# Three gate/up pages, not two, issued ahead of the next expert's upper down half

## The reference

```python
gu = xblk @ w_gate_up[e] + b_gate_up[e]              # (tokens, 1024) @ (1024, 2048)
x_glu = jnp.minimum(gu[:, :D_EXPERT], SWIGLU_LIMIT)
x_lin = jnp.clip(gu[:, D_EXPERT:], -SWIGLU_LIMIT, SWIGLU_LIMIT)
act = x_glu * jax.nn.sigmoid(SWIGLU_ALPHA * x_glu) * (x_lin + 1)
return act @ w_down[e] + b_down[e]                   # (tokens, 1024) @ (1024, 1024)
```

## Time and profile before

| | |
|---|---|
| median of 3 runs | 1222.7 us (1222.44 to 1223.84) |
| the profiled execution: its own time, its span | 1223.64 us, 1221.8 us |
| PE busy, DVE, ACT, POOL | 1032.7 us (85%), 289.0, 188.9, 31.6 |
| moved | 465.42 MB, 381 GB/s over the span |
| mean granted clock of TensorE | 0.943 |
| chain that ended last | PE 50%, DMA 39%, of which the down weights 35% |

### The profile page before, as it was taken

How to read it: one execution, slowest core, us unless ns; L and a number is a source line. 1 busy time by engine, 2 the same in 40 slices (tenths; PEclk the granted TensorE clock), 3 DMA queues, 4 the chain that set the end, 5 groups by cost and what they waited for, 6 DMA issues and landing times.

```text
span 1221.8 us, 21400 instructions
## 1 busy us (share of the span) xinstructions
PE 1032.7 (85%) x8279; PEld 504.9 (41%) x8280; DVE 289.0 (24%) x786; ACT 188.9 (15%) x459; POOL 31.6 (3%) x55
## 2 busy tenths in 40 slices
PE   2799999987785999979898899889888979696966
PEld 1565888743342334324443444334334333233333
DVE  6646522142121111202121212111211121111112
ACT  0311345041110101101110111111111111010102
POOL 1000200230000000000000000000000000000000
PEclk9799999997798999989998999999999999898989
DMA  9979730988999979999999999999999999999996
GB/s 352 385 272 402 292 135 6 407 316 351 426 425 426 426 288 380 425 426 418 411 423 425 403 427 425 425 401 426 425 427 396 427 426 427 423 426 425 425 426 259
DMA packets 60000, 465.42 MB, mean 381 GB/s; under 512 B 5342, under 2 KB 7430, under 8 KB 27084
## 3 DMA queue, kind: packets, MB, share of 16 engines
q1 hardware_dynamic: 59212, 462.50, 91.8%
q0 software_dynamic: 480, 1.59, 0.4%
q10 hardware_dynamic: 288, 1.05, 0.2%
HBM read 463.01 MB, written 2.11 MB: 381 GB/s over the span
## 4 chain that ended last, share of the span: by engine, by line
PE 50%; DMA 39%; DVE 5%; issue 3%; ACT 2%; POOL 1%; DVEq 0%; SPq 0%; ACTq 0%; POOLq 0%
DMA arena<-in_w_down_dram 35%; PE pp L1398 14%; PE pp L1427 14%; PE pp L1195 4%; DMA arena<-in_w_ada_dram 4%; PE pp L1117 2%; PE pp L1362 2%; PE pp L1208 2%; PE po L1260 2%; PE po L1343 2%; DVE arena L757 2%; PE pp L1371 1%; PE pp L1377 1%; ACT work L674 1%; PE po L1075 1%
## 5 line engine op out<-in xcount | busy, mean ns | idle before, releaser
L1398 PE MATMUL pp<-arena,work 128*32 128x256 f32 (+1 forms) x3840 | 376.5, 448 | 20.3 <-ACT work L674 20.3
L1427 PE MATMUL pp<-arena,work 128*32 128x256 f32 (+1 forms) x1920 | 205.8, 477 | 78.6 <-DMA arena<-in_w_down_dram 78.6
L1398 PEld LDWEIGHTS pp<-arena,work 128*32 128x32 f32 (+1 forms) x3840 | 165.9, 118 | 214.8 <-issue 129.8
L1427 PEld LDWEIGHTS pp<-arena,work 128*32 128x32 f32 (+1 forms) x1920 | 80.4, 128 | 185.6 <-DMA arena<-in_w_down_dram 90.9
L979 DVE TENSOR_SCALAR work<-pp 128x128 f32<-128x128 f32 (+1 forms) x74 | 24.9, 337 | 405.3 <-PE pp L1398 405.3
L1362 PE MATMUL pp<-h_sb,work 128*32 128x256 f32 (+1 forms) x480 | 59.6, 461 | 36.0 <-issue 31.5
L677 ACT ACTIVATE work<-work 128x128 f32<-128x128 f32 (+1 forms) x74 | 25.9, 350 | 405.3 <-DVE work L979 405.3
L973 DVE COPY work<-pp 128x256 f32<-128x256 f32 (+1 forms) x37 | 19.4, 525 | 255.2 <-PE pp L1362 255.2
L1343 PE MATMUL po<-work 64*128 64x512 f32 x304 | 75.5, 615 | 1.2 <-ACT work L693 1.2
L1195 PE MATMUL pp<-arena 128*128 128x256 f32 x256 | 57.4, 382 | 0.0
L757 DVE SCALAR_TENSOR_TENSOR arena<-arena,small 128x1024 f32<-128x1024 f32 x42 | 54.0, 1285 | 8.5 <-DMA arena<-in_w_ada_dram 7.0
(11 more groups left out here) (208 smaller groups left out, 650.2 us busy)
## 6 DMA issues: line engine op xcount, KB each, us to landing
arena<-in_w_gate_up_dram SPq DMA_DIRECT2D x128, 2048.0 KB, 26.8
arena<-in_w_down_dram SPq DMA_DIRECT2D x64, 2048.0 KB, 24.5
arena<-in_w_ada_dram SPq DMA_DIRECT2D x12, 2048.0 KB, 12.5
arena<-in_w_in_dram SPq DMA_DIRECT2D x5, 2048.0 KB, 15.5
arena<-in_w_gate_dram SPq DMA_DIRECT2D x4, 2048.0 KB, 14.3
arena<-in_w_out_dram SPq DMA_DIRECT2D x2, 2048.0 KB, 10.0
arena<-in_w_branch_a_dram SPq DMA_DIRECT2D x1, 2048.0 KB, 18.6
arena<-in_w_branch_b_dram SPq DMA_DIRECT2D x1, 2048.0 KB, 17.4
```

Source lines behind the costliest of these rows:

```text
L1398: mm = t_.matmul(pp[j * m:(j + 1) * m, UP[hh], 0:w].rearrange("p (s f) -> p s f", s=2), hgT[:, at:at + m], gu_w[slot][:, k, :, r * PAIR:(r ...
L1427: mm = t_.matmul(pp[j * m:(j + 1) * m, UP[0], 0:w], actT[:, at:at + m], wd[:, j * w:(j + 1) * w], start=(n == 0), stop=(n == KD - 1))
```

## The change

In each pass of SP's loop the third gate/up page (number 2) of place n + 2 is issued before the wait for the end of place n, behind a wait of its own for that page to be free, and no longer after the upper down half of place n + 1. The number of transfers and their sizes are the same. Nothing else is changed; the issues ahead of the loop and after it are as they were.

```diff
@@ -428,12 +428,13 @@
                     load_gu(slot, e, 0)
                     sp.wait_ge(s_gfree, total * 3 + 1)
                     load_gu(slot, e, 1)
+                    sp.wait_ge(s_gfree, total * 3 + 2)
+                    load_gu(slot, e, 2)
                     sp.wait_ge(s_y, total)
                     load_dhi(last_e)
                     sp.reg_mov(dhi_expert, e)
                     load_bgu(slot, e)
-                    for q in range(2, 4):
-                        load_gu(slot, e, q)
+                    load_gu(slot, e, 3)
                     load_dlo(slot, e)
                     count_blocks(i * 2 + (1 + slot))
```

## The result

1239.41 us (median of 4, 1238.71 to 1239.69) against 1223.27 us for the kernel before (4 runs): ratio 1.0128, 95% interval 1.0115 to 1.0140. The change makes the kernel 16.1 us slower; 1240.7 was forecast. The profiled execution has a span of 1237.4 us, 15.6 more than before.

A forecast was written before the change was run, and what follows sets the result against it. The expert loop was taken to stream weight pages at 4.98 us each, PE waiting for hi; 4.3 + 14.0 + 0 − 0.3 = +18.0 us on 1222.7 gave 1240.7 us, range 1234 to 1246.

The forecast's parts named there:

- Term 1: From place 3 on, each hi (upper down half) lands one page later in the queue: +4.3 us.
- Term 2: Places 9, 13, 17, 21: a new 4.0 us dry stretch of the queue, +3.5 us each, +14.0 us in all.
- The cycle's bounds: Delay per dry stretch in places 9, 13, 17, 21: 2.8 us if cheap, 4.2 us if slow.
- term 4: At the end, the last hi comes early against PE, so the last block's remaining wait goes: −0.3 us.
- Term 3: Place 5: the first gap grows to 7 us, the second shrinks to about 5, hi(6) as today: 0.

## Why the prediction was right

*Term 1 (4.3).* hi(3) lands 4.2 us later than before; the last eight passes, undone, give 4.8 back. That 4.2 meets 4.3 to a tenth is partly luck. The two traces differ by 1.2 us before the change has done anything: hi(0), issued ahead of the loop, lands at 276.52 + 12.1 = 288.6, and at 275.60 + 11.8 = 287.4 before. How much of this is in the 4.2 isn't shown, so the term is known to about 1 us.

*Term 2 (14.0).* From hi(9) to hi(10) 33.6 us instead of 30.3. The landings of the other three pairs give 33.8, 33.75 and 33.7 where the kernel before has 30.4, 30.35 and 30.3; the four add 13.6. The sum's two numbers were 11.14 us from hi to the issue of g0 (now 11.15) and 7.7 us for a page from an empty queue (7.7 again). The estimate of 6.8 us, from the fit in the Trainium skill (DMA: Bandwidth & Descriptors, Anatomy of one DMA) for transfers issued by GpSimd, isn't what SP's queue shows. The cycle's bounds were 2.8 and 4.2; the prediction doesn't say how it gets 2.8, and its upper sum of 21.8 leaves out term 4.

*Term 3 (0).* hi(5) lands at 405.57 + 24.17 = 429.74; hi(6) is issued at 463.70 into an empty queue and lands 7.8 us later, 41.8 us after hi(5), as before. The gaps were to be 7 and 5, and are 6.2 and 4.3.

*Term 4 (−0.3).* There is no wait in the last down product any more, its 64 products run through:

```profile
1221.99 3.66 PE L1428 MATMUL pp<-arena,work 128*32 128x256 f32 x64
```

They end at 1225.65, where those of before ended at 1210.14, +15.5.

What the sum has too much is 1.9 us on the median. The terms measured, 4.2 + 13.6 − 0.3 = 17.5, come 2 us above the +15.5 at the end of the last product. The difference lies in the streaming stretches between: each of the five from one hi to a later one (3 to 5, 10 to 13, 14 to 17, 18 to 21, 22 to 30) took 0.3 to 0.6 us less than before, 1.8 together (6 to 9 took 0.1 more). A page time of 4.98 for both orders was assumed there; in this trace it is slightly less, and I have no cause for it.

Two forecasts of the profile were off. PE's wait for hi grew to 92.6 and not 97. The largest part of what is missing is at place 3, where it grew by 1.7 us and not by 4.3, since PE was itself 2.5 us later there: y(2), which releases hi(3), is at 352.32 instead of 349.86.

```profile
370.48 4.49 PE L1428 MATMUL pp<-arena,work 128*32 128x256 f32 x48 [3.12 <-DMA arena<-in_w_down_dram]
```

The waits at places 12, 16, 20 and 24 grew by 4.8, 4.7, 3.1 and 3.3 us, where 3.5 each was forecast. And y(3) came at 375.18 instead of 373.6, since 48 products after the longer wait in place 3 took 4.49 us and not 2.80; it cost nothing, for hi(4) is bound by the queue.

## What to carry to other kernels

In one ordered queue that is full, a transfer issued earlier is another one that lands later. Before moving one ahead, look at who waits for the transfer that it passes, and at what stands behind that one while the next page's buffer is still in use; the gain comes only where the queue is about to run dry and the passed transfer has slack. Here the page issued early cost 16 us in all passes and gained some 7 to 8 in five of them, chosen by a number that the program has at hand.

## What was not expected of the hardware

A second queue did not get half of the bytes: a 2 MB page issued by ScalarE beside SP's queue landed after 18.7 us (median of 31), against 7.7 us from an empty queue and some 13 at an even share. The packets in the trace of that kernel say where it goes. The first packet of hi starts 3.6 us after the issue. From 4 to 13 us after the issue ScalarE's queue moves 163 GB/s and SP's 264, a share of 0.38, though the two start nearly as many packets of 8 KB and more (5025 and 4477 over 28 of the transfers): those of hi are of 8 KB, and most of SP's, the gate/up pages, of 16 KB. That the share of the bytes follows from the size of the packets fits these counts, but no run changed the size. Splitting hi over both queues or issuing it sooner wasn't tried either.

In the kernel with the even passes alone, after a wait of 6.26 us for hi in a wide place, the granted clock of the following tail was 0.65 and its time 8.20 us, where it took 5.37 after 0.99, in a place where that tail decides when a buffer comes free.
